# A fused two-block forward pass, one core: first units of the norms in two passes, GpSimd's low parts in smaller blocks, output weights split earlier, one copy moved

## The reference

```python
def first_block(x, ...):
    h = rms_norm(x, norm_mix_pre)
    z = h @ w_in                                  # RWKV, NSA and gate columns
    o_a = rwkv7_time_mix(z_rwkv, ...)             # 16 heads of 64, a scan over time
    o_b = nsa_attention(z_nsa, ...)               # 16 heads: compressed, selected, window
    g_a, g_b = split(sigmoid(z_gate), 2)
    m = g_a * (o_a @ w_branch_rwkv) + g_b * (o_b @ w_branch_nsa)
    x = x + rms_norm(m @ w_out, norm_mix_post)
    u = causal_dwconv(rms_norm(x, norm_ffn_pre) @ ffn_up, ...)
    return x + rms_norm((silu(u_gate) * u_val) @ ffn_down, norm_ffn_post)

def second_block(x, ...):
    x = x + even_mixer(rmsnorm(x, attn_norm[0]))  # stick-breaking (8 heads), sliding window with sinks (8)
    x = x + swiglu(rmsnorm(x, ffn_norm[0]))
    x = x + mla_mixer(rmsnorm(x, attn_norm[1]))   # 16 heads, low-rank q and kv, rotary parts
    x = x + swiglu(rmsnorm(x, ffn_norm[1]))
    return rmsnorm(x, final_norm)
```

## Time and profile before

| what | value |
|---|---|
| median of three runs | 1356.03 us (1354.17 to 1358.76) |
| the profiled execution: its own time | 1358.64 us |
| its span in the profile | 1356.8 us |
| mean granted TensorE clock | 0.99 |
| ScalarE, VectorE, GpSimd busy | 672.3, 890.0, 231.2 us |
| DMA | 189.90 MB, 140 GB/s on average |

### The profile page before, as it was taken

The page is one execution under the profiler, slowest core; times in us unless marked ns, Lnnn a source line. Parts: engine busy times, 40 slices in busy tenths (PEclk is TensorE's granted clock), DMA queues, the critical chain, the costliest instruction groups (busy, mean ns, idle before and its releaser), DMA issues.

```text
span 1356.8 us, 26559 instructions
## 1 busy us (share of the span) xinstructions
PE 1299.1 (96%) x10058; PEld 1145.8 (84%) x10058; DVE 890.0 (66%) x1726; ACT 672.3 (50%) x1282; POOL 231.2 (17%) x326
## 2 busy tenths in 40 slices
PE   7999999989889999999999989999999999999997
PEld 6888998878789988999988866888888976888886
DVE  5677877747656586788746556766646665766644
ACT  4455555543246645766535446544434566544433
POOL 0002222221344311232301000122200000122200
PEclk9999999999899999999999999999999999999999
DMA  7312112114311144555555412455554622455552
GB/s 314 125 66 93 65 64 69 59 65 171 138 63 63 65 176 164 179 176 182 189 202 179 155 63 94 154 185 185 187 187 156 216 95 67 151 186 185 186 186 93
DMA packets 26771, 189.90 MB, mean 140 GB/s; under 512 B 2960, under 2 KB 3088, under 8 KB 4400
## 3 DMA queue, kind: packets, MB, share of 16 engines
q1 hardware_dynamic: 25632, 182.55, 37.3%
q0 software_dynamic: 1040, 5.96, 1.5%
HBM read 186.40 MB, written 1.05 MB: 138 GB/s over the span
## 4 chain that ended last, share of the span: by engine, by line
PE 82%; DVE 7%; ACT 5%; issue 2%; DVEq 2%; DMA 1%; POOL 1%; POOLq 0%; ACTq 0%; SPq 0%
PE ps L594 35%; PE ps L622 12%; PE ps L540 10%; PE ps L624 6%; PE ps L857 3%; DVE ring_r L1959 2%; ACT early_r L1349 1%; PE ps L706 1%; PE ps L695 1%; DMA ring<-in_weights 1%; PE ps L565 1%; PE ps L874 1%; PE ps L763 1%; ACT xn L1393 1%; PE ps L572 1%
## 5 line engine op out<-in xcount | busy, mean ns | idle before, releaser
L1426 ACT ACTIVATE w_hi<-ring 128x1024 fp32r<-128x1024 f32 x125 | 132.6, 1061 | 306.9 <-PE ps L594 163.2
L622 PE MATMUL ps<-h_both,w_hi 128*128 128x512 f32 x704 | 249.3, 399 | 0.4 <-DVE h_both L1942 0.4
L1972 DVE TENSOR_TENSOR w_lo<-ring,w_hi 128x1024 fp32r<-128x1024 f32 x125 | 155.2, 1242 | 132.9 <-ACT w_hi L1426 132.7
L624 PE MATMUL ps<-h_both,w_lo 128*128 128x256 f32 x704 | 197.7, 281 | 0.0
L594 PE MATMUL ps<-h_both,w_hi 128*128 128x256 f32 x1008 | 182.9, 284 | 0.5 <-DVE h_both L1942 0.5
L622 PEld LDWEIGHTS ps<-h_both,w_hi 128*128 128x128 f32 x704 | 132.3, 188 | 34.6 <-issue 1.2
L594 PEld LDWEIGHTS ps<-h_both,w_hi 128*128 128x128 f32 x1008 | 156.9, 192 | 3.5 <-issue 3.4
L1978 DVE TENSOR_TENSOR w_lo<-ring,w_hi 128x1024 fp32r<-128x1024 f32 x125 | 157.2, 1258 | 0.0
L540 PE MATMUL ps<-oT_r,ring_r 128*128 128x256 f32 x512 | 145.6, 284 | 0.0
L594 PE MATMUL ps<-h_both,w_lo 128*128 128x256 f32 x504 | 142.6, 283 | 0.0
L624 PEld LDWEIGHTS ps<-h_both,w_lo 128*128 128x128 f32 x704 | 133.0, 189 | 0.0
(11 more groups left out here) (425 smaller groups left out, 2886.4 us busy)
## 6 DMA issues: line engine op xcount, KB each, us to landing
ring<-in_weights SPq DMA_DIRECT2D x170, 1024.0 KB, 4.8
arena<-in_aux POOLq DMA_DIRECT2D x1, 2112.0 KB, 12.7
grow<-in_rows POOLq DMA_DIRECT2D x3, 512.0 KB, 4.1
cst<-in_consts SPq DMA_DIRECT2D x1, 1497.5 KB, 15.2
x<-in_x SPq DMA_DIRECT2D x1, 1024.0 KB, 5.0
arena<-in_swbias POOLq DMA_DIRECT2D x1, 1024.0 KB, 7.4
arena<-arena POOLq DMA_DIRECT2D x1, 1024.0 KB, 9.5
out<-xn SPq DMA_DIRECT2D x4, 256.0 KB, 2.3
```

The costliest lines, as they stand in the source:

```text
L622: pe.matmul(bank[:].rearrange("p (a t) -> p a t", a=2), hi, h_both[:, :, k, :], start=k == 0, stop=False)
L624: m = pe.matmul(bank[:, 0:S], lo, h_hi[:, k, :], start=False, stop=k == KT - 1)
L1426: act.activation(w_hi[:, half_of(u0, m), WH:], ring[:, (u0 + m) % RING, WH:], ACT.Copy).then_inc(w_hi_p, 1)
L1972: dve.tensor_tensor(w_lo[:, half_of(u0, m), WH:], ring[:, (u0 + m) % RING, WH:], w_hi[:, half_of(u0, m), WH:].bitcast(F32), ALU.subtract). ...
```

## The change

- The norms transpose into ps[4] to ps[7], and the five products behind the transposes are gone. The first unit after each of the five norms runs in two passes (`first_unit`): for all k and both tiles first high weights and low weights by `h_hi`, waiting for `hi_out`, then high weights by `h_lo`, waiting for `lo_out`. In the feed-forward parts of the second block the 512 wide products of this one unit become two of 256 columns.
- GpSimd makes low parts in blocks of 256 columns. In the NSA attention the two halves of a unit stand behind two heads in a row. Unit ONE+3 is split ahead of the phase end, on ScalarE and on GpSimd.
- `take_u(n, 2)` stands ahead of the second `high_half`.
- `out_weights` splits the first unit at s = 3 (even) and s = 2 (MLA) instead of 4, once the unit before it is done, and the second at s = 6 on ScalarE and 7 on VectorE.
- In MLA the 13 products are gone, and the maximum of head 0 stands ahead of the split of unit 8 on VectorE.

The diff, cut to its core:

```diff
@@ -505,11 +505,10 @@
                     for k in range(KT):
                         if b == 1 and k == KT // 2:
                             pe.wait_ge(xn_act, r + 1)
-                        m = pe.transpose(ps[k // 2][:, (k % 2) * S + b * P:(k % 2) * S + b * P + P],
+                        m = pe.transpose(ps[4 + k // 2][:, (k % 2) * S + b * P:(k % 2) * S + b * P + P],
                                          xn[:, b, k * P:(k + 1) * P], ident)
                         if b == 1 and k % 2:
                             m.then_inc(xT_mm, 1)
-                idle_products(5, ps[7])
...
-            def input_ready(r):
-
-                def wait(k):
+            def first_unit(r, dsts, half):
+
+                for k in range(KT):
+                    if k % 2 == 0:
+                        pe.wait_ge(hi_out, 4 * r + k // 2 + 1)
+                    for tile in range(2):
+                        hi, lo = [t[:, half, k * S + tile * P:k * S + (tile + 1) * P] for t in (w_hi, w_lo)]
+                        dst, apart_lo = dsts[tile]
+                        pe.matmul(dst, hi, h_hi[:, k, :], start=k == 0 and (tile == 0 or apart_lo is not None), stop=False)
+                        pe.matmul(dst, lo, h_hi[:, k, :], start=False, stop=False)
+                for k in range(KT):
                     if k % 2 == 0:
                         pe.wait_ge(lo_out, 4 * r + k // 2 + 1)
-
-                return wait
+                    for tile in range(2):
+                        hi = w_hi[:, half, k * S + tile * P:k * S + (tile + 1) * P]
+                        dst, apart_lo = dsts[tile]
+                        if apart_lo is None:
+                            m = pe.matmul(dst, hi, h_lo[:, k, :], start=False, stop=k == KT - 1 and tile == 1)
+                        else:
+                            m = pe.matmul(apart_lo, hi, h_lo[:, k, :], start=False, stop=k == KT - 1)
+                return m
...
-                unit(0, 0, before=input_ready(2 * n_ffn))
+                unit_split(f"ffn{n_ffn}", 0)
+                first_unit(2 * n_ffn, [(ps[tile][:, 0:S], ps[tile][:, S:2 * S]) if n_ffn else
+                                       (ps[0][:, tile * S:(tile + 1) * S], None) for tile in range(2)],
+                           0).then_inc(unit_done, 1)
...
-            def split_f_unit(bank, name, m, before=None):
+            def split_f_unit(bank, name, m, r=None):
 
                 unit_split(name, m)
+                if r is not None:
+                    first_unit(r, [(bank[:, tile * S:(tile + 1) * S], None) for tile in range(2)],
+                               (m + 1) % 2).then_inc(unit_done, 1)
+                    return
...
-            def mla_idle(s):
-
-                if s == 2:
-                    pe.wait_ge(kv_out, 5)
-                    idle_products(13, ps[3])
...
@@ -1408,7 +1414,7 @@
                 for q in range(4):
                     act.wait_ge(xT_mm, 4 * r + q + 1)
                     for k in (2 * q, 2 * q + 1):
-                        m = act.activation(h_hi[:, k, :], ps[q][:, (k % 2) * S:(k % 2 + 1) * S],
+                        m = act.activation(h_hi[:, k, :], ps[4 + q][:, (k % 2) * S:(k % 2 + 1) * S],
                                            ACT.Copy, scale=gain[:, k:k + 1])
...
-            def out_weights(u0, s, s0=0):
-
-                if s in (s0, s0 + 1):
-                    act.wait_ge(unit_done, u0)
-                    split_unit(u0, s - s0)
+            def out_weights(u0, s, s0):
+
+                if s in (s0, 6):
+                    act.wait_ge(unit_done, u0 - 1 if s == s0 else u0)
+                    split_unit(u0, int(s > s0))
...
@@ -1671,10 +1677,10 @@
                     high_half(2 * n + 8, True)
                 if powers:
                     take_powers(n + 1, 3)
+                if scan:
+                    take_u(n, 2)
                 if n + 3 < PAIRS:
                     high_half(2 * n + 8, False)
-                if scan:
-                    take_u(n, 2)
...
             take_mixer(1)
+            split_one(ONE + 3)
             phase_end(act)
-            split_one(ONE + 3)
...
-                out_weights(U["even_out"], s, 4)
+                out_weights(U["even_out"], s, 3)
...
-                out_weights(U["mla_out"], s, 4)
+                out_weights(U["mla_out"], s, 2)
...
-            def out_weights(u0, name, s, s0=0):
-
-                if s in (s0 + 1, s0 + 2):
-                    split_unit(u0, name, s - s0 - 1)
+            def out_weights(u0, name, s, s0):
+
+                if s in (s0 + 1, 7):
+                    split_unit(u0, name, int(s == 7))
...
+            def mla_max(s):
+
+                dve.wait_ge(a_scores, H + s + 1)
+                softmax_max(s % 3, ps[s % 2], const("causal")[:, 0:P], const("causal")[:, P:KEYS])
+
+            mla_max(0)
             split_unit(down, "mla", 8)
             for s in range(H + 3):
-                if s < H:
-                    dve.wait_ge(a_scores, H + s + 1)
-                    softmax_max(s % 3, ps[s % 2], const("causal")[:, 0:P], const("causal")[:, P:KEYS])
+                if 0 < s < H:
+                    mla_max(s)
...
+            def low_half(m, first):
+
+                pool.wait_ge(one_hi_p if first else one_hi_d, m + 1)
+                pool.sem_inc(apart, 1)
+                for c in range(WH if first else 0, UNIT if first else WH, 256):
+                    part = slice(c, c + 256)
+                    lo = pool.tensor_tensor(one_lo(m)[:, part], ring[:, one_unit(m) % RING, part],
+                                            one_hi(m)[:, part].bitcast(F32), ALU.subtract)
+                if not first:
+                    lo.then_inc(one_lo_e, 1)
+
             def split_one(m):
 
-                for rows, signal in ((slice(WH, UNIT), one_hi_p), (slice(0, WH), one_hi_d)):
-                    pool.wait_ge(signal, m + 1)
-                    pool.sem_inc(apart, 1)
-                    lo = pool.tensor_tensor(one_lo(m)[:, rows], ring[:, one_unit(m) % RING, rows],
-                                            one_hi(m)[:, rows].bitcast(F32), ALU.subtract)
-                lo.then_inc(one_lo_e, 1)
+                low_half(m, True)
+                low_half(m, False)
...
             split_one(ONE + 2)
+            split_one(ONE + 3)
             phase_end(pool)
 
-            due = {0: [1]}
+            due = {}
             for n in range(2, 7):
-                due.setdefault((mixer_step(n) + 1) // 2, []).append(n)
+                for later in range(2):
+                    due.setdefault((mixer_step(n) + 1) // 2 + later, []).append((n, not later))
             for h in range(H):
                 pool.wait_ge(max_ready, NSA0 + 2 * h - 2)
                 pool.sem_inc(apart, 1)
                 pool.tensor_tensor(b_st[:, h % 2, :], dist, const("slope")[:, h:h + 1].broadcast_to((P, KEYS)),
                                    ALU.mult).then_inc(b_staged, 1)
-                for n in due.get(h, ()):
-                    split_one(ONE + 2 + n)
-            for h in range(H, H + 2):
-                for n in due.get(h, ()):
-                    split_one(ONE + 2 + n)
+                for n, first in due.get(h, ()):
+                    low_half(ONE + 2 + n, first)
+            for h in range(H, H + 3):
+                for n, first in due.get(h, ()):
+                    low_half(ONE + 2 + n, first)
             phase_end(pool)
```

More of the change, by code:

```diff
@@ L585, in attention, with split_product @@
                                   stop=True).then_inc(o_mm, 1)
-            def split_product(dst, pairs, first=True, last=True, before=None):
+            def split_product(dst, pairs, first=True, last=True):
                 for n, (l, r) in enumerate(pairs):
                     for a, b in ((0, 0), (0, 1), (1, 0)):
-                        if before is not None and a == b:
-                            before(n)
                         m = pe.matmul(dst, l[a], r[b], start=first and n == 0 and a == b,
@@ L609, in ffn_up, with unit @@
                 h = (h_hi, h_lo)
-                def unit(j, i, before=None):
+                def unit(j, i):
                     pe.wait_ge(ff_act if n_ffn else ff_conv, 4 + n_ffn * FT + 4 * i + j - 3)
@@ L618, in unit @@
                         for k in range(KT):
-                            if before is not None and tile == 0:
-                                before(k)
                             hi, lo = [t[:, j % 2, k, tile * P:(tile + 1) * P] for t in w]
@@ L627, in unit @@
                                           [([t[:, j % 2, k, tile * P:(tile + 1) * P] for t in w],
[L628 to L629 removed]
+                                            [t[:, k, :] for t in h]) for k in range(KT)])
                     m.then_inc(unit_done, 1)
[L632 removed]
+                unit_split(f"ffn{n_ffn}", 0)
+                first_unit(2 * n_ffn, [(ps[tile][:, 0:S], ps[tile][:, S:2 * S]) if n_ffn else
```

(12 more changed lines are left out.)

11 lines of the change are left out of this document (4 added, 7 removed).

## The result

The changed kernel took 1332.96 us (median of four runs, 1332.21 to 1336.67), the kernel before 1355.12 in the same comparison: the ratio is 0.9833, with a 95% interval of 0.9813 to 0.9852. The forecast was 1336.9, in a range of 1332.0 to 1346.5; the result lies in the range, 1.0 above its fast end, and at the edge of the 1333 to 1341 that the forecast gave as its own.

What follows compares the result with a forecast made beforehand. PE was busy 1299.1 of 1356.8 us, so only its waits or lower clock could be won. Terms 4.3 + 3.9 + 1.9 + 4.6 + 4.4 = 19.1 took the profiled 1358.64 to 1339.5; median forecast 1336.9, range 1332 to 1346.5.

Steps and rivals of the forecast that it cites:

- Norms: At the five norms PE starts after one pair of high parts: 1.0 us a norm, 4.3 in all, bounds 0 and 6.2.
- The cover: At the norms, unit 1's low half is ready at 536.88, before unit 0 ends at 537.4: half a microsecond to spare.
- cost nothing; their going saves nothing: The 5 products after each norm's transposes stand in an idle moment, so removing them gains 0.
- u copy: In five RWKV phases the copy starts 0.97 earlier and PE's wait of 0.76 goes: 3.9 us, bounds 0 and 4.0.
- GpSimd's low parts: NSA attention: shorter holds by GpSimd win 2.95, a later phase end costs 1.05; net 1.9 us, bounds -1.1 and 3.
- a unit costs between 4.7 and 5.8: GpSimd's time for one unit in 256 column blocks, from columns only to 8 x 0.73; 5.6 us was taken.
- rival 2: Slower: half clock for 10.2 us at each of five norms loses 5.1 each time; net 6.5 slower, 1362.5; chance 0.03.
- rival 4: In RWKV and NSA the next wait takes the place of the removed one: 5.8 goes, 1342.7; chance 0.14.
- The moved unit: Unit ONE+3 ahead of the phase end before the NSA attention: the phase ends 0.9 to 1.1 us later, 1.05 taken.
- Even attention: Earlier output weight split: PE's wait 0.4 instead of 3.52, half clock behind it gone; 4.6 us, bounds 0 and 5.2.
- MLA: MLA attention: 13 products, a 2.49 wait and half clock go, some given back; 4.4 us, bounds 0 and 7.4.
- Rival 1: The clock falls where the removed products stood, at five norms and MLA: 10.2 us given back, 1347; chance 0.10.

Runs made afterwards that it cites:

- e3: The kernel before with only GpSimd's 256 column blocks, halves behind two heads, unit ONE+3 still behind head 0: 1348.68 us.
- e5: The kernel before with only the even attention's output weights split earlier, at s = 3 and 6 (VectorE one step later): 1352.50 us.
- e8: The kernel before with all three MLA edits (earlier output weights, 13 products gone, maximum of head 0 ahead of unit 8's split): 1348.54 us.
- e9: The changed kernel with the five products of 512 columns put back behind each norm's transposes: 1335.59 us.
- e7: The kernel before with only the 13 products ahead of the MLA heads removed: 1354.53 us.
- e1: The kernel before with only the norms' edits (two-pass first units, transposes into ps[4] to ps[7], five products gone): 1356.49 us.
- e4: The kernel before with only unit ONE+3 split ahead of the phase end on ScalarE and GpSimd, in blocks of 1024: 1357.27 us.

## Why the prediction was right, and where it was not

- **Norms, right** in mechanism and size (4.4 for 4.3). The cover over unit 1's low half held, the fourth norm gave little (0.36), and the norms with narrow products gave 0.98 each, those without 1.05. That the five products "cost nothing; their going saves nothing" was right of the kernel before and wrong of the new order: kept, they would have cost 0.49 a norm.
- **u copy, right**: 4.4 for 3.9; the step is 0.9, more than the wait of 0.76 that the forecast took. From `scan_u` to `scan_state` it was 2.07 (192.28 to 194.35) and is 1.14 (187.71 to 188.85); the wait in brackets counts only from the end of the row before.
- **GpSimd's low parts: the sum missed a place.** The step "a unit costs between 4.7 and 5.8" was applied to the units in the attention only. Unit ONE+2, ahead of it, was not costed at all, though the earlier trace rows stood in the text as rival 2's example of a low clock. The two VectorE rows of 2.31 and 1.96 were there to be read; L2437's 1.88 was read as a single case. It was worth 3.1 of wait, and 2.9 of half clock behind it. Without this place the term would not have come to its 1.9: the instances gave 2.5 for 2.95, the phase end took 2.0 of that, and 0.5 was left, near rival 4's nothing. With it the term came to 6.4, beyond its upper bound of 3.
- **The moved unit, sized wrong**: it cost 2.0 at the phase end where 1.05 was taken. GpSimd took 6.5 for the unit, and VectorE's L2410 and L2415 took 0.18 and 0.16 longer beside it. The Trainium skill says it more sharply than the forecast used it (SBUF — State Buffer, "SBUF: two separate sides"): the pair of ports that VectorE and GpSimd share is a lock that one instruction has until it ends, and VectorE wants it for two SBUF inputs or in a 2-port mode. The traces agree for two SBUF inputs (L2394 took 2.31). L2404, with one SBUF tile as its input, waited 1.8 too, which fits if it ran in a 2-port mode; no trace shows the mode. The reduction and the copy from PSUM did not wait.
- **Even attention, sized wrong**: "unit 1 at s = 6 and 7 is wanted only at s = 10" asked when PE wants it, and not what stands behind it in VectorE's order. That cost 1.4. Wait (0.17 for 0.4) and clock (1.4 for 1.5) came as forecast.
- **MLA, sized wrong**: of the gains of 7.4, 7.1 came (the half clock gave 1.4); given back were 1.0, not 2.95. The wait of 1.4 laid out for s = 5 was 0.79; of the 0.4, the 0.7 and the 0.45 for unit 8, only a 0.23 is seen.
- **The clock.** Rival 1 had the sign wrong for the whole: with fewer and shorter waits of PE the estimate for half clock fell from 13.4 to 6.0, where the forecast counted 3.2. At the places of the edits 5.7 of it can be read (2.9 ahead of the NSA attention, 1.4 in each of the other two). The edits at the waits did that (by the estimate e3 3.4, e5 2.1, e8 3.4, each with a standard error of about 1). The products taken out cost no clock: e9, which has 25 of them back, has 5.7, and e7, without the 13, fell by 1.2. What e1 lost to half clock stays open.

The forecast's 19.1, with 5.9 for the missed place, +1.6 in MLA, +0.5 and +0.1 for u copies and norms, and -1.2, -1.0, -0.5 for even attention, phase end and instances, makes 24.5; the rest of 26.4 is chance stretches and the start. Between medians it is 22.2. The forecast was 3.9 too slow: some 3.1 by the gain, and 0.9 since the median of the kernel before came out at 1355.12 and not 1356.03.

That the sum holds is in part luck. The errors of the other terms cancel to 0.5, and the 5.9 of a place that the text did not cost brought the result within 1.0 of the end of the range.

## What to carry to other kernels

Look for instructions that take many times their usual duration beside a long one of GpSimd, everywhere, not only where the change is: cutting GpSimd's work into short blocks was worth more than any rearrangement in the stages that wait for it. Where an instruction is moved earlier, ask what now stands behind it on its own engine. And cost a wait of TensorE with the half clock that may follow it. A gain of a few us can stay invisible in the full time, as the norms' 4.5 did in ten runs of e1, since the same program's runs differ by such stretches; the distance of single instructions between two profiles showed it.

## What was not expected of the hardware

- VectorE waits for the end of a whole GpSimd instruction: 2.31 for 0.28, 1.96 for 0.17, with blocks of 2.35; 0.70 and 0.35 with blocks of 0.72. A reduction beside a long block and a copy from PSUM beside a short one kept their 0.26 and 0.41. It works both ways: GpSimd's blocks beside a 1.22 us subtraction took 1.76 (for 0.72, changed kernel) and 3.38 (for 2.37, e4).
- Stretches of half clock lasted 3.4, 6.8 or 10.2 us, apart from the one at each profile's end. From 285 us on each began in a wait of PE or at most 1.1 us behind one, and they were surer with longer waits: with 4.85 in 8 of the 8 profiles that have this wait, with 3.52 in 8 of 8, with 2.49 in 5 of 7, with 2.29 (at 286 in the changed kernel, where PE was busy through the whole stretch) in 11 of 14, with 1.78 in none of 6. The wait's length alone does not settle it: at 28.7 and 1069.8 in the kernel before PE waited only 0.46 and 0.59, after 32 products of 48 columns and 20 of 2. In the same place, ahead of any edit, they stood in some profiles and not in others, and the mean clock of the kernel before went from 0.987 to 0.994 between its runs.
- In the profiles of e3, e4 and e5 the products of the last feed-forward part follow one another faster between 1174 and 1288 (by the kernel before): a pair of one wide and one narrow takes 0.347 on average in place of 0.353, 2.2 us in all, at full clock and where no edit reaches. The table's places don't include it; why it comes, and if other executions have it, is open.
